# One layer of a hybrid diffusion step: the scores moved in between the turned pieces of probabilities, the output stores moved to another queue, and a table of row numbers widened

## What is computed

```python
def gqa_block(qb, k, v):                       # 8 query heads, 2 key heads, width 64
    s = einsum('bqhgd,bshd->bhgqs', qb, k) * HEAD_DIM ** -0.5
    return einsum('bhgqs,bshd->bqhgd', softmax(s), v)

def diff_block(qb, k, v, lam):                 # 4 heads, two 64-wide maps each, values 128 wide
    p = softmax(einsum('bqhmd,bshmd->bhmqs', qb, k) * HEAD_DIM ** -0.5)
    return einsum('bhqs,bshe->bqhe', p[:, :, 0] - lam[None, :, None, None] * p[:, :, 1], v)

x = x + gate1 * m                              # m: both branches, projected, gated, summed, projected
h = rms_norm(x, g_ffn) * (1.0 + scale2) + shift2
x = x + gate2 * expert_choice_ffn(h, ...)      # 16 experts, each takes its top tokens, SwiGLU
y_prompt, y_sample = rms_norm(xp, g_final), rms_norm(xs, g_final)
```

## Time and profile before

| | |
|---|---|
| time, median of 3 runs | 1306.68 us (1304.41 to 1308.26) |
| profiled execution, its own time | 1306.07 us |
| its span, first to last instruction | 1304.2 us |
| busy over the span | PE 91%, DVE 70%, ACT 55%, POOL 14% |

### The profile page before, as it was taken

How to read it: one execution, slowest core, us unless ns; L and a number is a source line. 1 busy time by engine, 2 the same in 40 slices (tenths; PEclk the granted TensorE clock), 3 DMA queues, 4 the chain that set the end, 5 groups by cost and what they waited for, 6 DMA issues and landing times.

```text
span 1304.2 us, 17235 instructions
## 1 busy us (share of the span) xinstructions
PE 1186.0 (91%) x6017; PEld 853.1 (65%) x6017; DVE 913.9 (70%) x1137; ACT 718.2 (55%) x1013; POOL 186.6 (14%) x154
## 2 busy tenths in 40 slices
PE   4899978988879999999849999999999999999991
PEld 1678766767756777767546666766676666766650
DVE  2773627887847143154588999979996999979972
ACT  2532236666643212211647777767766777677761
POOL 2234220000000000010120111101114211101113
PEclk9999989998989999999969999999999999999996
DMA  9932231011051534453519999799988999899964
GB/s 374 323 105 66 79 78 39 24 31 31 1 214 59 178 126 153 164 206 129 215 60 317 370 377 378 273 341 386 379 293 307 368 378 381 271 325 385 376 258 171
DMA packets 109079, 293.19 MB, mean 225 GB/s; under 512 B 29089, under 2 KB 30322, under 8 KB 108738
## 3 DMA queue, kind: packets, MB, share of 16 engines
q1 hardware_dynamic: 103392, 268.57, 56.4%
q0 software_dynamic: 4528, 15.67, 4.5%
q10 hardware_dynamic: 1074, 7.91, 1.6%
HBM read 270.48 MB, written 16.38 MB: 220 GB/s over the span
## 4 chain that ended last, share of the span: by engine, by line
PE 82%; DVE 7%; DMA 5%; ACT 2%; issue 2%; POOL 1%; SPq 0%; DVEq 0%; POOLq 0%; ACTq 0%
PE ps L1070 13%; PE ps L1071 13%; PE ps L1072 13%; PE ps L662 9%; PE ps L663 9%; PE ps L664 9%; PE ps L844 3%; PE ps L860 2%; DVE neg_max L1658 2%; DMA x_dram<-y_g,rows_e 2%; DMA raw<-in_w_mod_dram 1%; PE ps L883 1%; PE ps L684 1%; PE ps L1025 1%; PE ps L1026 1%
## 5 line engine op out<-in xcount | busy, mean ns | idle before, releaser
L1748 DVE TENSOR_TENSOR raw_lo<-raw,w_hi 128x1024 fp32r<-128x1024 f32 x256 | 304.4, 1219 | 39.4 <-ACT w_hi L1412 31.4
L1412 ACT ACTIVATE w_hi<-raw 128x1024 fp32r<-128x1024 f32 x252 | 265.2, 1061 | 82.5 <-PE ps L1072 81.7
L1070 PE MATMUL ps<-w_hi,xe_hi 128*80 128x512 f32 x512 | 204.4, 399 | 3.6 <-DVE raw_lo L1748 1.8
L1072 PE MATMUL ps<-w_hi,xe_lo 128*80 128x512 f32 x512 | 202.5, 395 | 0.0
L2174 POOL DMA_INDIRECT x_dram<-y_g,rows_e x16 | 95.1, 5943 | 520.5 <-DVE y_g L1977 520.5
L1748 DVE TENSOR_TENSOR extra_lo<-extra,w_hi 128x1024 fp32r<-128x1024 f32 x128 | 152.5, 1219 | 8.3 <-ACT w_hi L1412 7.6
L1412 ACT ACTIVATE w_hi<-extra 128x1024 fp32r<-128x1024 f32 x128 | 136.3, 1065 | 39.5 <-PE ps L1072 39.0
L662 PE MATMUL ps<-w_hi,ht_hi 128*128 128x512 f32 (+1 forms) x350 | 136.7, 390 | 5.9 <-DMA ht_lo<-ht_dram 5.9
L663 PE MATMUL ps<-raw_lo,ht_hi 128*128 128x512 f32 (+1 forms) x350 | 134.2, 383 | 0.0
L664 PE MATMUL ps<-w_hi,ht_lo 128*128 128x512 f32 (+1 forms) x350 | 134.2, 383 | 0.0
L470 ACT ACTIVATE w_hi<-raw 128x1024 fp32r<-128x1024 f32 x50 | 50.8, 1055 | 136.1 <-DMA raw<-in_w_in_dram 55.5
(11 more groups left out here) (285 smaller groups left out, 1974.2 us busy)
## 6 DMA issues: line engine op xcount, KB each, us to landing
raw<-in_w_exp_down_dram SPq DMA_DIRECT2D x112, 512.0 KB, 6.6
raw<-in_w_exp_gate_dram SPq DMA_DIRECT2D x80, 512.0 KB, 5.3
extra<-in_w_exp_up_dram SPq DMA_DIRECT2D x64, 512.0 KB, 5.4
raw<-in_w_exp_up_dram SPq DMA_DIRECT2D x64, 512.0 KB, 5.4
raw<-in_w_mod_dram SPq DMA_DIRECT2D x24, 1024.0 KB, 8.3
extra<-in_w_exp_gate_dram SPq DMA_DIRECT2D x48, 512.0 KB, 5.4
raw<-in_w_in_dram SPq DMA_DIRECT2D x17, 1024.0 KB, 5.4
extra<-in_w_exp_down_dram SPq DMA_DIRECT2D x16, 512.0 KB, 5.2
```

The costliest lines, as they stand in the source:

```text
L1070: pe.matmul(b, stat_hi, hi[:, cols], start=(k == 0), stop=False)
L1072: mm = pe.matmul(b, stat_lo, hi[:, cols], start=False, stop=(k == KD - 1))
L1412: act.activation(w_hi[:, (DENSE_SPLITS + h) % NHL, :], expert_half(h), ACT.Copy)\
L1748: dve.tensor_tensor(expert_lo_half(h), expert_half(h), w_hi[:, (DENSE_SPLITS + h) % NHL, :].bitcast(F32), ALU.subtract).then_inc(s_lo, 1)
```

## The change

Three edits.

1. In a query slot PE turns only the first piece of probabilities ahead of the two `scores`, and the others behind them. DVE does its two `row_max` ahead of the copy of its piece there. Other slots are as before.
2. `rows_e` has a column for each of the 16 experts, and DVE no longer waits for the scatters before it writes a group's four.
3. The five output stores are issued by SP, behind its loads; POOL keeps only the `one_over_rms`.

```diff
+QUERY_SLOTS = {PREP[m] for m in range(2, MAPS)}
...
-        rows_e = sb("rows_e", [P, EG], U32)
+        rows_e = sb("rows_e", [P, NE], U32)
...
             for t in range(NT):
                 sp.dma_start(x_f[:, t, :], x1_dram[t * P:(t + 1) * P, :]).then_inc(s_x[t], 16)
+            ys = y_sample[0].rearrange("(t p) d -> t p d", p=P)
+            for t in range(NT):
+                sp.wait_ge(s_fy, t + 1)
+                sp.dma_start(ys[t] if t < NTL else y_prompt[0], x_f[:, t, :]).then_inc(s_yout, 16)
+            sp.wait_ge(s_yout, 16 * NT)
...
-            def turn_probs(i):
-                p, t = PUS[i]
-                per = KTL if t < NTL else 1
-                for n in P_PIECES[i]:
+            def turn_probs(i, pieces):
+                for n in pieces:
+                    p, t = PUS[i]
+                    per = KTL if t < NTL else 1
                     tiles = PIECES[n][2]
...
-                if 0 <= i - LAG < len(PUS):
-                    turn_probs(i - LAG)
+                pieces = P_PIECES[i - LAG] if 0 <= i - LAG < len(PUS) else []
+                early = 1 if i in QUERY_SLOTS else len(pieces)
+                turn_probs(i - LAG, pieces[:early])
                 if i + 1 < len(PUS):
                     scores(2 * i + 2)
                     scores(2 * i + 3)
+                turn_probs(i - LAG, pieces[early:])
...
-                if 0 <= i - LAG < len(PUS):
+                if 0 <= i - LAG < len(PUS) and i not in QUERY_SLOTS:
                     probs_turned(i - LAG)
                 if i + 1 < len(PUS):
                     row_max(2 * i + 2)
                     row_max(2 * i + 3)
+                if 0 <= i - LAG < len(PUS) and i in QUERY_SLOTS:
+                    probs_turned(i - LAG)
...
-                    if not first:
-                        dve.wait_ge(s_scat, 16 * EG * i)
-                    dve.tensor_copy(rows_e[0:EROWS, :], table.rearrange("p (e c) -> p e c", e=EG)[:, :, NE])\
+                    dve.tensor_copy(rows_e[0:EROWS, bass.ds(EG * i, EG)], table.rearrange("p (e c) -> p e c", e=EG)[:, :, NE])\
                        .then_inc(s_rows, 1)
...
-                pool.indirect_dma_start(x1_dram[:, :], bass.IndirectOffsetOnAxis(ap=rows_e[0:EROWS, e:e + 1], axis=0),
-                                        y_g[0:EROWS, e % 2, :], None, compute_op=ALU.add).then_inc(s_scat, 16)
+                pool.indirect_dma_start(x1_dram[:, :], bass.IndirectOffsetOnAxis(ap=rows_e[0:EROWS, n:n + 1], axis=0),
+                                        y_g[0:EROWS, n % 2, :], None, compute_op=ALU.add).then_inc(s_scat, 16)
...
-            for t in range(NT + 1):
-                if t < NT:
-                    pool.wait_ge(s_fss, t + 1)
-                    one_over_rms(rs[:, t:t + 1], ss[:, t:t + 1], D, s_frs)
-                if t == 0:
-                    continue
-                t -= 1
-                pool.wait_ge(s_fy, t + 1)
-                pool.dma_start(ys[t] if t < NTL else y_prompt[0], x_f[:, t, :]).then_inc(s_out, 16)
-            pool.wait_ge(s_out, 16 * (2 + NT))
+            for t in range(NT):
+                pool.wait_ge(s_fss, t + 1)
+                one_over_rms(rs[:, t:t + 1], ss[:, t:t + 1], D, s_frs)
+            pool.wait_ge(s_out, 32)
```

More of the change, by code:

```diff
@@ L356, in build @@
         s_slot = [sem(f"s_slot{n}") for n in range(ESLOT)]; s_xct = sem("s_xct")
-        s_ids = sem("s_ids"); s_slots = sem("s_slots"); s_rows = sem("s_rows"); s_yg = sem("s_yg"); s_scat = sem("s_scat"); s_gfin = sem("s_gfin")
+        s_ids = sem("s_ids"); s_slots = sem("s_slots"); s_rows = sem("s_rows"); s_yg = sem("s_yg"); s_scat = sem("s_scat"); s_gfin = sem("s_gfin"); s_yout = sem("s_yout")
         s_hi = sem("s_hi"); s_lo = sem("s_lo"); s_half = sem("s_half")
@@ L2166, in scatter @@
             def scatter(n):
-                e = n % EG
                 pool.wait_ge(s_yg, n + 1)
@@ L2183, in _ @@
             pool.wait_ge(s_scat, 16 * NE)
-            ys = y_sample[0].rearrange("(t p) d -> t p d", p=P)
-            for t in range(NT + 1):
-                if t < NT:
-                    pool.wait_ge(s_fss, t + 1)
-                    one_over_rms(rs[:, t:t + 1], ss[:, t:t + 1], D, s_frs)
-                if t == 0:
-                    continue
-                t -= 1
-                pool.wait_ge(s_fy, t + 1)
-                pool.dma_start(ys[t] if t < NTL else y_prompt[0], x_f[:, t, :]).then_inc(s_out, 16)
-            pool.wait_ge(s_out, 16 * (2 + NT))
+            for t in range(NT):
+                pool.wait_ge(s_fss, t + 1)
+                one_over_rms(rs[:, t:t + 1], ss[:, t:t + 1], D, s_frs)
+            pool.wait_ge(s_out, 32)
 _INS = ["x_prompt", "x_sample", "cache_attn_k", "cache_attn_v", "cache_diff_k", "cache_diff_v", "c", "c_ctx",
```

## The result

The changed kernel takes **1296.31 us** (median of 14 runs, 1292.96 to 1303.86), the kernel before, timed beside it, 1305.01 us (14 runs, 1302.5 to 1308.26). The ratio is 0.9934, with a 95% interval of 0.9918 to 0.995: 8.6 us shorter, 6.5 to 10.7 by the interval. The forecast was 1294, range 1291 to 1300.5. The profiled execution took 1293.16 us, its span 1291.2.

What follows compares the result with a forecast made beforehand. PE's own work was taken to bound 700 to 1275 us, and waits, chiefly PE's for `query_lo`, the attention stage. Gains 2.2 + 3.15 + 3.3 + 3.0 + 0.55 + 0.3 = 12.5 us gave about 1294 us, range 1291 to 1300.5.

Steps and rivals of the forecast that it cites:

- Waits of the attention stage: Query slots: PE's waits for `query_lo` fall from 19.2 us to under 6; gains of 2.2, 3.15 and 3.3 us.
- first pair: Query slots 2 and 3, without output block: 2.2 us gained, about 1.0 of it from scores that ran at half speed.
- plain pairs: Query slots 7/8, 12/13, 17/18: about 1.05 us gained a pair, 3.15 us in all.
- differential ones: Three later query-slot pairs, such as 27/28, with DVE as full as PE: 1.10 us gained in slot 27, 3.3 in all.
- Clock: TensorE's granted clock behind slots 23 and 28: both falls, about 1.5 us each, expected to go, 3.0 us; the shakiest term.
- half speed stays or comes elsewhere: Rival: half-speed stretches remain or move, so only 8.5 us gained, 1298 us; chance 0.25 for 1296 to 1301.
- falls in new places: Sign of being wrong: TensorE's granted clock falls in new places in the changed profile.
- Row numbers: Expert stage: DVE's 6.2 us wait for a scatter goes, 0.55 us gained, at least 0 and at most 1.
- Tail: Last loop: period stays 2.02 us; last store by SP changes time by -1.0 to +0.3, taken as -0.3 us.
- my own: Forecast case: waits and half-speed stretches gone, 1291 to 1296 us; chance 0.57.
- The wait moving on: Rival: p1 and p2 wait later, copies and `y_t` hold the values; only 4 to 5 us gained, 1302; chance 0.09.
- ACT's queue: Rival: in query slots p1's copy delays the exponentials and closes a cycle, 7 us slower, 1313; chance 0.04.

Runs made afterwards that it cites:

- doubled work: Changed kernel with p0 transposes of slots 23, 28, 33 and context scores of 23, 28, 33, 38 made twice: 1290.3 us, ratio 0.9892.
- the run with the plain pairs alone: Kernel before with the new order only in query slots below 20 (2, 3, 7, 8, 12, 13, 17, 18): 1298.2 us, ratio 0.993.
- early values: Changed kernel; in query slots ACT's output block goes ahead of turned probabilities, PE's values of the last turned tile ahead of late pieces: 1288.0 us, ratio 0.9868.
- the order alone: Kernel before with only the first edit, the order in query slots on PE and DVE: 1299.9 us, ratio 0.9958.

## Why the prediction was right, point by point

**Waits of the attention stage: right.** The cleanest comparison is between two profiles with the same half-speed stretches behind the stage's start, one near 205 us and none behind a pair: the old order takes 178.0 us, the new one with its doubled work 169.5. That is 8.5 us. (In the stage's first microseconds the second one stands at half speed 2 us longer, which can hide at most 1 us of gain.) The first profiles say the same: before has three stretches and after four, and less 1.4 us for each they take 176.9 and 168.1 us, 8.8 apart. My 2.2 + 3.15 + 3.3 = 8.65 held 1.0 for half speed in the first pair, and in both these runs that stretch is there; without it I had 7.65. Taken apart by the run with the plain pairs alone, less 1.5 us for each of its two stretches: 178.0 - (176.4 - 3.0) = 4.6 us for the first and the plain pairs (forecast 4.35), and 8.5 - 4.6 = 3.9 for the differential ones (forecast 3.3). The wait left for `query_lo` is 6.6 us, where I wrote under 6, and in slot 7 it is gone, as laid out. The stage as a whole is 7.4 us shorter in its first profile and not 9 to 12, since the clock's part of that sum failed.

**Clock: wrong.** The step that failed is "by my layout about half of that after, and I expect both falls to go: 3.0 us". They became more. All five profiles of kernels with the whole new order and neither doubled work nor early values have a stretch behind each of the three differential pairs, fifteen of fifteen places; the four with the old order there have 2, 0, 0 and 1, three of twelve. At 1.4 us each the new order pays 4.2 us where the old pays about 1.1. Behind the pairs the term is -3 and not +3, and it takes back most of the differential pairs' 3.9 us. Counted from 200 us to the stage's end, wherever they stand, the five profiles with the new order have 3.6 stretches each and the three with the whole old order 2.0, so over the stage the loss is nearer 2 us, an estimate from few profiles. The timed runs point the same way. The mean granted clock of the order alone is 0.959 over 6 executions, of the kernel before beside it 0.965 over 11; with the new order in the plain pairs alone it is 0.966 over 6, beside 0.962 over 11. And the times, 1298.2 us with the new order in the plain pairs alone and 1299.9 in all pairs, have overlapping intervals: what the differential pairs gain in waits doesn't show. What I did see, that slots 32 and 33 had the same waits and no fall, should have kept me from giving the falls a sign at all. The rival that I wrote down, half speed stays or comes elsewhere, is what happened, and falls in new places stood on my own list of signs that I am wrong. Why the clock falls there stays open.

**Row numbers: not shown.** DVE's wait is gone, as forecast; 0.55 us is too small for these runs to confirm or refute.

**Tail: mis-sized.** The period stayed, as forecast. The last store's part, from DVE's end to the landing, fell from 3.3 us to 2.6, by 0.7 where I took 0.3: 0.3 by the earlier start and 0.4 by the shorter transfer. By the Trainium skill's page "DMA: Bandwidth & Descriptors", section "Specifications", the transfer's part would be 0.4 too, an estimate. But the whole term was 4.7 us, not 0.3. I asked how the last store gets from issue to landing, and not what lies between its landing and the end of the span. The earlier trace rows had it: 1296.77 + 3.0 = 1299.8, and the span ends at 1304.2. Those 4.4 us had no row, so I took them as fixed.

**The sum.** Forecast 12.5 us; measured 8.6. In the profiles the attention stage is 180.2 us in the mean of the three with the whole old order and 174.0 in the five with the new: 6.2 us, which is the waits' 8.5 less about 2 for the clock, and with the tail's 4.7 it is 10.9, just above the interval's end of 10.7. Where 2 us of that go in the timed runs, if they do, stays open; the spread of the expert stage is larger. The forecast came out within 2.3 us by luck: two errors, about 6 us in the clock and 4.4 in the tail, had opposite signs, and the kernel before measured 1305.0 us in 14 runs where my sum started from 1306.7 in 3. As a difference it was 3.9 us off, and 12.5 lies outside the interval of 6.5 to 10.7.

**Rivals.** The time, 1296.3 us, fell into the case that I gave 0.25, half-speed stays, and not into my own with 0.57. Its 8.5 us agree with the measured 8.6 by the same luck: it had nothing of the tail's 4.4 us. The wait moving on was half right for the second slots, where 5.9 us were still to be had, as the early values showed. ACT's queue closed no cycle: slot 7 has PE, DVE and ACT each earlier than before.

## What to carry to other kernels

Work that doesn't need a bank belongs in front of work that waits for one, but look at both ends of the chain: a further gain as large as the whole change (1296.3 to 1288.0 us), 5.9 us of it waits and the rest clock, came from moving the values and the output block that stood behind the wait that the profile named first. Account for the whole span up to its last microsecond: here the 4 us between the last landing and the end belonged to POOL's program, and most of them were hidden by giving SP the last wait. And a granted clock that falls in some executions can't be booked as a gain from a change of order; look at several profiles before you give it a sign.

## What the runs showed of the hardware

- From POOL's last wait to the end of the span it takes about 4 us (4.4 in the kernel before, 3.9 in two other runs, one in which POOL stored nothing). Where SP has the last wait and POOL is long done, it is 0.1. The profile has no row for it.
- A tiny POOL instruction (128 x 1, 0.19 us at its least) lasts 1.28 us when it starts with DVE's scaling of 1.28 us, in the changed kernel in the last three periods of five, and ends 0.05 us behind it. That agrees with the shared port of the Trainium skill's page "SBUF — State Buffer", section "SBUF: two separate sides". The period fell only when POOL left the loop, from 2.00 to 1.39 us.
- Half speed behind differential pairs came fifteen times in fifteen with the new order, three in twelve with the old, although PE stood less, and vanished when 28 matmuls were added. What tells these apart stays open.
- The expert stage varies by 7 us (538.2 to 545.2) between executions of the same work; no cause was looked for.
